# Twelve units of an attention take their softmax between the matmuls of the values' projection, and three engines share the rest anew

## What is computed

```python
a = rmsnorm(h, ln_pre_mix)
q, k, v, u, z = split(a @ w_in)                    # 512 columns each
attn = dilated_attention(q, k, v)                  # 8 heads of 64; causal, a bias by distance
u, z = gelu(u), layernorm(gelu(z))                 # the gating unit
mixed = einsum('gij,bnjgc->bnigc', tril(w_s), z_chunks) + b_s
sgu = u * mixed
groups = concatenate([rmsnorm(attn), rmsnorm(sgu)])
h = h + rmsnorm(groups @ w_out)
...
cond = silu(c)                                     # the second block
mod = cond @ ada_w + ada_b                         # 96 columns of 128 values
```

## Time and profile before

| | |
|---|---|
| median of three runs | 2014.75 us |
| the profiled execution | 2013.93 us, span 2012.1 us |
| mean granted clock of TensorE | 0.983 of full speed |
| end of q's tiles, mixing matmuls | 81.26 to 84.83 us |
| v's matmuls | 107.71 to 129.57 us |
| first scores | 132.24 us |
| end of the last unit's outputs | about 173.9 us |
| ada columns beside k and v | twelve |

### The profile page before, as it was taken

The page is one execution under the profiler, slowest core; times in us unless marked ns, Lnnn a source line. Parts: engine busy times, 40 slices in busy tenths (PEclk is TensorE's granted clock), DMA queues, the critical chain, the costliest instruction groups (busy, mean ns, idle before and its releaser), DMA issues.

```text
span 2012.1 us, 26799 instructions
## 1 busy us (share of the span) xinstructions
PE 1951.8 (97%) x9346; PEld 1572.3 (78%) x9354; DVE 1080.2 (54%) x1649; ACT 564.8 (28%) x1126; POOL 1209.6 (60%) x681
## 2 busy tenths in 40 slices
PE   9989999999999899999999999999999999999999
PEld 7866788888887777777788888877766678888887
DVE  6775569877786515454434333144976544343322
ACT  4045310000125225562311121132356522111210
POOL 7650688887665566655666666745650057666664
PEclk9999999999999899999899999989999999999999
DMA  7430277766542131114222333212220024322331
GB/s 271 154 129 1 73 252 251 251 235 211 193 162 64 63 105 43 49 41 163 82 96 94 95 100 97 94 53 95 74 74 1 1 63 120 99 94 94 97 102 63
DMA packets 62326, 221.16 MB, mean 110 GB/s; under 512 B 6907, under 2 KB 7163, under 8 KB 62124
## 3 DMA queue, kind: packets, MB, share of 16 engines
q1 hardware_dynamic: 45216, 161.71, 25.6%
q10 hardware_dynamic: 17036, 58.46, 8.1%
HBM read 218.00 MB, written 2.14 MB: 109 GB/s over the span
## 4 chain that ended last, share of the span: by engine, by line
PE 91%; DVE 4%; ACT 2%; issue 1%; DMA 1%; POOL 1%; ACTq 0%; SPq 0%; DVEq 0%; POOLq 0%
PE bank L305 25%; PE bank L307 25%; PE bank L306 25%; PE bank L809 2%; PE bank L337 2%; PE bank L342 2%; PE bank L338 2%; PE bank L427 2%; PE bank L632 1%; PE bank L768 1%; PE bank L819 1%; PE bank L644 1%; PE bank L657 1%; PE bank L1314 1%; DVE y L1704 1%
## 5 line engine op out<-in xcount | busy, mean ns | idle before, releaser
L1153 POOL TENSOR_TENSOR w_lo<-raw,w_hi 128x1024 fp32r<-128x1024 f32 (+1 forms) x304 | 767.9, 2527 | 24.8
L305 PE MATMUL bank<-a_hi,w_hi 128*128 128x512 f32 x1960 | 766.1, 391 | 5.0 <-DVE tmp L1862 1.9
L307 PE MATMUL bank<-a_hi,w_lo 128*128 128x512 f32 x1960 | 763.8, 390 | 0.0
L306 PE MATMUL bank<-a_lo,w_hi 128*128 128x512 f32 x1960 | 763.6, 390 | 0.0
L1148 POOL TENSOR_SCALAR w_hi<-raw 128x1024 fp32r<-128x1024 f32 x298 | 349.3, 1172 | 583.9 <-PE bank L307 361.4
L305 PEld LDWEIGHTS bank<-a_hi,w_hi 128*128 128x128 f32 x1960 | 368.4, 188 | 83.5 <-issue 2.8
L307 PEld LDWEIGHTS bank<-a_hi,w_lo 128*128 128x128 f32 x1960 | 368.4, 188 | 77.1
L306 PEld LDWEIGHTS bank<-a_lo,w_hi 128*128 128x128 f32 x1960 | 368.5, 188 | 76.0
L1704 DVE CUSTOM_DVE_ANT_0 y<-y,cond 128x1024 f32<-128x1024 f32 x96 | 222.4, 2351 | 4.6 <-DMA y<-in_ada 4.5
L1719 DVE SCALAR_TENSOR_TENSOR tmp<-bank,vecs,tmp 128x511 f32<-128x511 f32 x88 | 66.0, 749 | 260.9 <-ACT tmp L1421 260.9
L1421 ACT ACTIVATE tmp<-bank,vecs 128x512 f32<-128x512 f32 x88 | 68.3, 779 | 372.9 <-PE bank L307 364.8
(11 more groups left out here) (261 smaller groups left out, 2224.0 us busy)
## 6 DMA issues: line engine op xcount, KB each, us to landing
raw<-in_stream SPq DMA_DIRECT2D x299, 512.0 KB, 3.5
y<-in_ada ACTq DMA_DIRECT2D x96, 512.0 KB, 4.5
x<-in_x SPq DMA_DIRECT2D x4, 512.0 KB, 6.7
bias<-in_bias ACTq DMA_DIRECT2D x1, 2048.0 KB, 14.2
y<-rel_rows ACTq DMA_DIRECT2D x1, 2048.0 KB, 8.4
bias<-rel_rows ACTq DMA_DIRECT2D x1, 2048.0 KB, 16.1
out<-x SPq DMA_DIRECT2D x8, 256.0 KB, 2.0
cond<-in_c ACTq DMA_DIRECT2D x1, 512.0 KB, 6.9
```

Source lines behind the costliest of these rows:

```text
L305: pe.matmul(o, lhs_hi, rhs_hi, start=start, stop=False, **kw)
L306: pe.matmul(o, lhs_hi, rhs_lo, start=False, stop=False, **kw)
L307: return pe.matmul(o, lhs_lo, rhs_hi, start=False, stop=stop, **kw)
L1153: m = pool.tensor_tensor(w_lo[:, s, part], raw[:, j, part], f32(w_hi[:, s, part]), ALU.subtract)
```

## The change

TensorE's list: the mixing matmuls write banks 4, 5, 3, 4, and k waits for the third addition to them; the sum of squares of the gating unit comes ahead of v; v no longer waits for all four banks but for each; twelve units' scores (banks 4, 6, 5, 7) and the transposes of units 0 to 3 stand between v's matmuls. After v, units 4 to 17 are transposed in a schedule that catches up (`A_CATCH_UP`), and units 12 to 31 go as before. VectorE's list: columns lie between the tiles of q and of k, with `cond` read from PSUM; the first twelve units are masked, inverted and scaled by VectorE out of PSUM, the others are masked and inverted by VectorE and scaled by GpSimd; VectorE copies the odd units' transposes from unit 5 on, ScalarE the others. The weights of a unit lie in a ring of twelve buffers rather than eight. ScalarE makes both table loads ahead of the first exponentials and empties v's banks after the first twelve exponentials and four copies.

```diff
+        A_FIRST, A_TURNED = 3 * TT, 4
+        A_FIRST_BANKS = (4, 6, 5, 7, 4, 6, 5, 7, 4, 6, 5, 7)
+        A_CATCH_UP = ([4], [5], [6, 7], [8], [9, 10], [11], [12, 13], [14], [15, 16], [17])
+        def a_turns(step):
+            if step >= A_FIRST + 10:
+                return [step - A_TURN] if step - A_TURN < len(a_units) else []
+            return A_CATCH_UP[step - A_FIRST]
+        def pe_first_units(pe, p):
+            if p % 2 == 0 and p <= A_FIRST:
+                first = p - 2
+                if first == 0:
+                    pe.wait_ge(inverse_step, 5 * inverse_index("sgu") + 1)
+                    pe.wait_ge(ada_done, ADA_STEP)
+                    pe.wait_ge(*freed("k", 4))
+                elif first >= 4:
+                    pe.wait_ge(a_sems["normed"], first - 2)
+                pe_scores(pe, first)
+            if p == 13:
+                pe.wait_ge(a_sems["normed"], 10)
+                pe_turn(pe, 0)
+                pe_turn(pe, 1)
+            if p == 15:
+                pe_turn(pe, 2)
+                pe_turn(pe, 3)
...
+            pe.wait_ge(a_sems["normed"], A_FIRST)
+            for step in range(A_FIRST, n + A_TURN + 2):
+                if step == A_FIRST:
+                    pe_turn(pe, 4)
                 if step < n and step % 2 == 0:
+                    if step == A_FIRST:
+                        pe.wait_ge(*freed("v", 2))
+                    elif step == A_FIRST + 2:
+                        pe.wait_ge(*a_copied(2))
+                    else:
+                        pe.wait_ge(a_sems["masked"], step - 2)
+                    pe_scores(pe, step)
+                if step == A_FIRST:
+                    pe.wait_ge(*freed("v", 4))
+                    pe.wait_ge(*a_copied(3))
+                    pe_outputs(pe, 1)
+                for u in a_turns(step):
+                    if u > 4:
+                        pe_turn(pe, u)
+                        if u % 2:
+                            pe_outputs(pe, u - 2)
+            pe_outputs(pe, n - 1)
...
+        def normalise(e, u):
+            cols = P * (a_units[u][1] + 1)
+            e.wait_ge(a_sems["rden"], u + 1)
+            e.tensor_scalar(a_weights(u)[:, 0:cols], a_exps(u)[:, 0:cols], rden[:, u:u + 1], None,
+                            ALU.mult).then_inc(a_normed(u)[0], 1)
...
+            for step in range(A_FIRST, n + A_TURN):
+                if step < n:
+                    dve_mask(v, step)
+                if A_FIRST <= step - A_NORM < n:
+                    dve_inverse_sum(v, step - A_NORM)
+                for u in a_turns(step):
+                    if u % 2:
+                        cols = P * (a_units[u][1] + 1)
+                        v.wait_ge(a_sems["turned"], u + 1)
+                        v.wait_ge(a_sems["out"], u - 3)
+                        v.tensor_copy(y[:, u % 4, 0:cols], a_turned(u)[:, 0:cols]).then_inc(a_sems["copied_odd"], 1)
...
-            split_stream(SPLIT, START["gu1"] + AHEAD)
+            split_stream(SPLIT, START["out1"] + SPLIT)
+            for u in range(A_FIRST, len(a_units)):
+                normalise(pool, u)
+            split_stream(START["out1"] + SPLIT, START["gu1"] + AHEAD)
...
             for g in range(GROUPS):
+                if g == 2:
+                    pe.wait_ge(*freed("q", 4))
                 if g == 3:
                     pe.wait_ge(mixed_step, 1)
                 for i in range(TT):
-                    m = pe.matmul(bank[5 + g % 3][:, i * P:(i + 1) * P], big[:, 16 + i, g * P:(g + 1) * P], ws[:, g, :],
+                    m = pe.matmul(bank[(4, 5, 3, 4)[g]][:, i * P:(i + 1) * P], big[:, 16 + i, g * P:(g + 1) * P], ws[:, g, :],
                                   start=True, stop=True)
                 m.then_inc(mixed_ready, 1)
+            pe.wait_ge(mixed_step, 3)
             pe_tiles(pe, "k")
             pe.wait_ge(masks_ready, 5)
-            pe_token_tiles(pe, "v")
+            pe.wait_ge(mixed_step, 4)
             pe_sum_group(pe, "sgu", 0)
-
-            pe.wait_ge(*freed("v", 4))
-            pe.wait_ge(mixed_step, 4)
-
-            pe.wait_ge(inverse_step, 5 * inverse_index("sgu") + 1)
+            pe_token_tiles(pe, "v", between=pe_first_units)
             pe_pairs(pe)
...
             a.activation(cond[:], cond[:], ACT.Silu).then_inc(cond_ready, 1)
+            a.wait_ge(cond_ready, 1)
+            for n in range(2):
+                a.activation(last_banks[:, n, :], cond[:, n * S:(n + 1) * S], ACT.Copy).then_inc(cond_ready, 1)
...
+            load_columns(0, 9)
             act_squares(a, "sgu", [big[:, 12 + c, :] for c in range(4)], lambda c: (sgu_ready, c + 1))
+            load_columns(9, ADA_STEP)
+            act_rms(a, "sgu")
+            a.preload_act_table(ACT.Exp)
+            act_first_units(a)
             for t in range(TT):
                 act_tile(a, "v", t, START["v"] + 3, big[:, 8 + t, :], scale=first_rstd[:, t:t + 1])
-            act_rms(a, "sgu")
...
+            columns(5, 6)
+            dve_add_square(v, "sgu", 1)
+            key_tile(0)
+            dve_add_square(v, "sgu", 2)
+            columns(7, 8)
+            dve_add_square(v, "sgu", 3)
+            key_tile(1)
+            columns(9)
+            key_tile(2)
+            columns(10, 11)
+            key_tile(3)
+            dve_diag(v, "sgu", add=False, wait=False)
```

More of the change, by code:

```diff
@@ L488, in attention @@
             sems = {k: sem(f"{name}_{k}") for k in
[L489 removed]
+                    ("scores", "scaled", "masked", "exp", "rden", "normed", "turned", "copied", "copied_odd", "normed_pool", "out", "evac")}
             units = [(2 * pair + side, i) for pair in range(heads // 2) for i in range(TT) for side in range(2)]
@@ new lines, in a_copied, with pe_scores @@
+        def a_copied(u):
+            if u < A_TURNED:
+                return a_sems["copied"], u + 1
+            return (a_sems["copied_odd"], u // 2 - 1) if u % 2 else (a_sems["copied"], A_TURNED + u // 2 - 1)
+        def pe_scores(pe, first):
+            for u in (first, first + 1):
+                h, i = a_units[u]
+                cols = P * (i + 1)
+                pe.matmul(a_scores(u)[:, 0:cols], big[half(h), h // 2, i * P:(i + 1) * P],
+                          big[half(h), 16 + h // 2, 0:cols], start=True, stop=True).then_inc(a_sems["scores"], 1)
@@ new lines, in pe_turn @@
+        def pe_turn(pe, u):
+            pe.wait_ge(*a_normed(u))
+            if u >= 2:
+                pe.wait_ge(*a_copied(u - 2))
+            for j in range(a_units[u][1] + 1):
+                m = pe.transpose(a_turned(u)[:, j * P:(j + 1) * P], a_weights(u)[:, j * P:(j + 1) * P], ident)
+            m.then_inc(a_sems["turned"], 1)
+        def pe_first_units(pe, p):
[15 more added lines that the diff above has]
+                pe_turn(pe, 3)
@@ L566, in pe_outputs @@
                         m.then_inc(sems["out"], 1)
-        def dve_pairs(v):
[L569 to L589, removed]
@@ L591, in act_pairs @@
-        def act_pairs(a):
[L592 to L614, removed]
@@ new lines, in dve_mask, with dve_inverse_sum @@
+        def dve_mask(v, u):
+            h, i = a_units[u]
+            cols = P * (i + 1)
+            v.wait_ge(a_sems["scores"], u + 1)
+            if u >= A_FIRST:
+                v.wait_ge(a_sems["turned"], u - A_FIRST + 1)
+            v.tensor_tensor_reduce(a_weights(u)[:, 0:cols], a_scores(u)[:, 0:cols], bias[:, h, S - cols:S],
+                                   -1.0, 3e38, ALU.add, ALU.min, neg_max[:, u:u + 1]).then_inc(a_sems["masked"], 1)
+        def dve_inverse_sum(v, u):
+            v.wait_ge(a_sems["exp"], u + 1)
+            v.reciprocal(rden[:, u:u + 1], den[:, u:u + 1]).then_inc(a_sems["rden"], 1)
@@ new lines, in act_exp, with act_copy @@
+        def act_exp(a, u):
+            cols = P * (a_units[u][1] + 1)
+            a.wait_ge(a_sems["masked"], u + 1)
+            a.activation(a_exps(u)[:, 0:cols], a_weights(u)[:, 0:cols], ACT.Exp, bias=neg_max[:, u:u + 1],
+                         scale=-1.0, accum_out=den[:, u:u + 1]).then_inc(a_sems["exp"], 1)
+        def act_copy(a, u):
+            cols = P * (a_units[u][1] + 1)
+            a.wait_ge(a_sems["turned"], u + 1)
+            if u >= 4:
+                a.wait_ge(a_sems["out"], u - 3)
+            a.activation(y[:, u % 4, 0:cols], a_turned(u)[:, 0:cols], ACT.Copy).then_inc(a_sems["copied"], 1)
@@ new lines, in act_first_units, with evacuate @@
+        def act_first_units(a):
+            for u in range(A_FIRST):
+                act_exp(a, u)
+            for u in range(A_TURNED):
+                act_copy(a, u)
+        def act_pairs(a):
+            n = len(a_units)
+            def evacuate(c):
+                a.wait_ge(a_sems["out"], 8 * c + 8)
+                a.activation(big[:, c, :], bank[6 + c % 2][:], ACT.Copy).then_inc(a_sems["evac"], 1)
+            for step in range(A_FIRST, n + A_TURN):
+                if step < n:
+                    act_exp(a, step)
+                for u in a_turns(step):
```

(5 more changed lines are left out.)

100 lines of the change are left out of this document (56 added, 44 removed).

## The result

The changed kernel takes 2019.74 us (median of eight runs, 2018.87 to 2021.40), the kernel before, beside it, 2014.82. The ratio is 1.0026, with a 95% interval of 1.0016 to 1.0037: slower by 5 us, where 2016.0 was forecast with a range up to 2019. The profiled execution took 2018.87 us, span 2017.1, against a span of 2012.1 before.

What follows compares the result with a forecast made beforehand. TensorE, busy 97% of the span, was taken as the bound. The stretch summed to 87.7 us against 89.1, 1.4 less; 3.2 of low clock in k made it 1.8 more: 2016.0 us, range 2010 to 2019.

Steps and rivals of the forecast that it cites:

- the duration of GpSimd's scaling: Units 12 to 31: 0.62 us at 512 columns, taken from a one-input operation of that size.
- Rival D: Behind v, TensorE waits for GpSimd's scaling: 6 us on top of A's 2016.0 less slack, 2020.5; chance 0.10.
- Waits behind v: TensorE waits 1.3 us just after v, then 2.4 to 2.5 us through the remaining units and tail.
- The wait ahead of k: Before k, TensorE waits for VectorE's third addition to the mixing results; cost 2.8 us, nothing to hide it.
- The clock in k: TensorE's clock falls to its lower level in k after the wait; cost 3.2 us (0 to 3.4).
- Twelve units inside v: Inside v: 4.75 us of work moved in, 1.0 us for eight changes of matmul kind, 0.5 us of waits.
- Columns: VectorE's ada columns beside q and k: 1.2 us each instead of 2.35, nothing on the path.
- No wait ahead of v: Before v, TensorE's wait of 1.1 us goes, since v starts on the first free bank.
- The clock behind v: After v, waits stay below a microsecond, so today's low stretch, 2.45 us, should go.
- The sum: From mixing matmuls' end to last outputs' end: 87.7 us against 89.1, plus 3.2 us of low clock in k.
- slower by over 0.2%: Whole kernel slower than 2018.8 us: D, some of E and A's tail; chance 0.15.

Runs made afterwards that it cites:

- the fast form: Changed kernel, wait ahead of k left in, with a second, constant factor of 1.0 in GpSimd's scaling: 2012.64 us, ratio 0.9994 to the kernel before.

## Why the prediction was wrong, point by point

- **The step that failed** is the duration of GpSimd's scaling: "I take 0.62, same kind". It measured 1.57 us at 512 columns. The 0.62 was that of an instruction with two constant factors; the changed kernel's has one factor, which differs by partition, and no second operation. I had the upper end, 1.29 from its two-input operations, and even that was too low; so was the estimate of 1.0 as twice VectorE's 0.49. Rival D, with chance 0.10, is what happened in its mechanism. That its 6 us come near the 6.4 here is partly luck: D counted waits alone, in seven pairs of units, and here 4.67 us are waits, in three pairs (20 and 21, 28 and 29, 30 and 31), and some 1.7 are low clock, which D did not have.
- **Waits behind v**: forecast 1.3 and then 2.4 to 2.5 us. The first measured 1.03 + 0.24. The second was 4.67 for GpSimd and 0.6 for ScalarE's copies. With the fast form there are still four waits, 2.3 us, for ScalarE's copies, so the sum of 2.5 would have been about right, but by luck: the waits I named, for the mask and the scaling, are not among them.
- **The wait ahead of k**: forecast 2.8, measured 2.64, with the first product held for 2.58 us, as I read it from the earlier trace rows.
- **The clock in k**: it fell, as forecast, but came back after 3 us of matmuls: 1.5 us lost against 3.2. The mistake was to take the length of another low stretch for this one, and all of it as matmuls: the one in the windows of the earlier trace rows is 6.8 us long, and TensorE works in 5.3 of them. This second error hid about a third of the 4.9 us that the working was short by behind v, so that 2016.0 is nearer to 2019.74 than the working behind v deserves. That the clock fell at all was less sure than the length of the wait made it seem. The 2.64 us lie midway between the two cases of the earlier trace rows, the clock fell in all five executions with a wait of 2.64 us ahead of k that have a trace (from 87.1 us here, in three of the others only from 89.2 or 89.3), and it did not fall behind the 3.15 us of the run with `cond` in SBUF. The length of the wait alone does not decide it.
- **Twelve units inside v**: forecast 21.8 + 4.75 + 1.0 + 0.5 = 28.05, measured 28.3. The parts are off in opposite ways: the waits came to 0.20 us in place of 0.5, and 28.3 - 21.8 - 4.75 - 0.2 leaves about 1.6 for the eight changes of kind, in place of 1.0.
- **Columns**: taken at 1.2 us, measured 1.20 to 1.22. The price was right and its working was not: 1.2 is half of 2.35, not a third, and the row of 0.749 us at 511 columns would have given 1.5 for 1024 in proportion. No wait ahead of v, as said.
- **The clock behind v**: "there the low stretch of today (2.45 us) should go". It went at that place and came back at 162 us, behind waits of 0.82 and 0.67 us for GpSimd. With the fast form there is none between v and the last outputs.
- **The sum**: 90.9 us forecast for the stretch (87.7 + 3.2), 94.2 measured. The differences: -1.7 for the clock in k, -0.2 for the wait, +0.3 in v, and behind v 39.0 against 34.1 (1.3 + 30.3 + 2.5), +4.9. Of these 4.9, 2.8 are waits (6.6 against 3.8), 1.7 the clock, and 0.4 more of work. With the fast form the changed kernel measured 0.9994, below the 1.0006 that 2016.0 stands for: with the right duration for GpSimd the forecast would have been too high, mostly by the 1.7 us of clock in k.

By the ratio of 1.0026 the outcome is slower by over 0.2%, which had a chance of 0.15; its interval, 1.0016 to 1.0037, reaches a little below that line.

## What to carry to other kernels

Before an operation goes to another engine, its duration must come from an instruction of exactly that form there, the number of its operations and the kind of its operands included; a row of the same name was off by two and a half times. A short operation that hides at 1.04 us can stop the bound engine at 1.57, with a mean load that still fits (8.7 us in a rhythm of 9.35), so compare the duration with the slack in that rhythm and not with the mean load alone. Put a wait for a buffer at the first instruction that writes it: one bank of four cost the whole phase its start, and moving the wait by three tiles gave about 3 us back.

## What the runs showed of the hardware

- GpSimd's `tensor_scalar` with one multiplication by a value of each partition takes 0.61, 0.92, 1.25 and 1.57 us at 128, 256, 384 and 512 float32 columns; with a second multiplication by 1.0 it takes 0.37, 0.48, 0.59 and 0.69 us. More work in the instruction, and at 512 columns less than half the time. Why is left open; no run here tried one operation with a constant, or other pairs of operations.
- Its product with a spread second tensor, 1.04 us at 512 columns, is faster too than the form with one operation.
- VectorE's 1024-column multiply and sum takes 1.2 us with its second input in PSUM, also across GpSimd's subtraction, and up to 3.4 us with it in SBUF across one (1.22 alone). The Trainium skill, page "SBUF — State Buffer", section "Who interferes with whom", says so of two inputs in SBUF beside a GpSimd instruction that reads SBUF; these runs agree, 3.42 us beside one against 1.22 alone.
- What a low stretch of TensorE's clock costs differs: 1.5 us behind the wait of 2.64 us ahead of k, 1.7 at 162 us in the changed kernel, 2.7 in the stretch from 132.8 to 139.6 us of the kernel before (TensorE works in 5.3 of its 6.8 us), 3.1 at 169 to 176 us with the wait at k's fourth tile.
- Whether the clock falls is not decided by the length of the wait ahead alone: it fell behind 2.64 us, and behind 0.82 and 0.67 us with short work between, and stayed at 2.4 GHz behind 3.15 us.
